# First block's feed-forwards: the first step as plain products in place of the seven-product scheme

## The chip, the cores and the metric

The kernel runs on one core of a Trainium2 chip. The metric is the device time of one execution in microseconds, taken over several runs. A core has a matrix engine (TensorE, PE), a vector engine (VectorE, DVE), an activation engine (ScalarE, ACT), a general engine (GpSimd, POOL) and a queue that starts most transfers (SyncE, SP). They run side by side and wait for one another by semaphores.

## The reference

A sequence of 512 tokens with 1024 channels goes through two blocks of two layers each. Every layer is a mixer (a gated delta rule, dilated window attention, sparse attention and others) and a feed-forward. The change touches the two feed-forwards of the first block, one after each of its mixers:

```python
def swiglu(h, w_in, w_out):
    gate, up = jnp.split(h @ w_in, 2, axis=-1)
    return (jax.nn.silu(gate) * up) @ w_out
...
h = (rms_norm(x, norm_ffn[layer]) * (1.0 + sc2) + sh2).astype(x.dtype)
x = x + g2 * swiglu(h, w_ffn_in[layer], w_ffn_out[layer])
```

`w_in` is 1024 x 5632 (2816 columns of gate and 2816 of up), `w_out` is 2816 x 1024, all in float32.

## The kernel before, in words

Activations are kept transposed: a tile is 128 channels (partitions) by 512 tokens, so `h` is 8 such tiles. The function `swiglu` (L1030) is one stage. Its first half makes 22 tiles of gate and 22 of up; its second multiplies by `w_out`. Weights come into two slots in turn (`c.slots[0]`, `c.slots[1]`); SP reloads a slot when the semaphore `done` says that TensorE has finished with it (L712). The weights of the first two steps are loaded in the stage before (`first_ffn_weights`).

**The seven products.** A step takes the weights of one tile of gate and one of up (both 1024 deep) and computes both tiles. Taken as a 2x2 by 2x2 product of blocks, this would be 8 block products; the class `SevenProducts` does it with 7, from sums of blocks of the weights and sums of blocks of `h` (a Winograd form of Strassen's scheme). Each block product is 4 matmuls of 256 columns, 28 a step, written out in `products` (L802 to L816; the matmul is L810) in the order P1, P2, P6, P7, P4, P5, P3. Who supplies what:

- P1 and P2 need only weights and `h` (in the first step TensorE waits for `h` tile by tile, semaphore `ready`).
- The sums of weights (`fold` in `gpsimd`, L735 to L741: four instructions a step) are made by POOL; P6 waits for them (`folded`).
- The sums of `h` (`sum_inputs`, L837 to L850) are made by DVE once in a stage: t1 (L844), t2 (L847), t3 (L848, written over the block b12 of `h` itself), t4 (L850). In the first step P6 waits for t2, P7 for t3, P4 for t4 (semaphore `t_in`).
- `combine` (L893 to L919) adds the seven products up on DVE into `gate` and `up`, as far as it can after P4 (`half_done`) and the rest after the step (`done`). The sums read PSUM banks 0 to 3 for even steps, 4 to 7 for odd ones.
- ACT takes the Silu of the gate (L1078), DVE multiplies it with up into `hidden` (L1114), and after each pair of steps adds sums of `hidden` (L885 to L890).

**Around the first step.** `Norm` makes `h`: TensorE spreads the inverse norm (L504), DVE scales tile by tile (L512), ACT adds the shift (L498). In the feed-forward of layer 0 alone there is extra work for the next mixer (`LayerAhead`): four small matmuls ahead of the first step (`make_rows`, L974), two copies and some transfers on ACT (L981, L985, L991), and multiplications of rows of `w_ada` on DVE (L1003, L1006) in the first eight pairs of steps. A semaphore `second_free` keeps the second step off the banks of `make_rows` until ACT has copied them.

The class already has a form for plain products in banks 0 and 1 (`whole_bank`), used by the second block's feed-forwards (L765), with `sum_inputs_early` (t1, t2, t4) and `sum_inputs_late` (t3, L870, after the plain steps have read `h`).

Of the kernel before, what the change touches and what calls it, by code (L numbers as in the profile page):

```python
# [18 lines left out]

F32 = mybir.dt.float32  # L20
ACT = mybir.ActivationFunctionType
LOG_AND_EXP, GELU = 6, 11
AX = mybir.AxisListType
ds = bass.ds

# [3 lines left out]
KT = D // P  # L29
# [19 lines left out]
FT = F1 // P  # L49
# [353 lines left out]
ADA_FIRST = 4  # L403
# [79 lines left out]
class Norm:  # L483
# [178 lines left out]
class SevenProducts:  # L662
# [18 lines left out]
    WHOLE = 2  # L681
# [44 lines left out]
    def landed_out(self, i, j):  # L726
        return i * (3 * 64) + (32 * self.KH + 64 * (j // 2 + 1))

    def gpsimd(self, pool, whole=False):

        c, nc = self.c, self.c.nc

        def fold(s, kc, before):
            b = lambda n: self.block(c.slots[s], n, kc)
            nc.gpsimd.tensor_tensor(b(self.S1), b(self.A21), b(self.A22), ALU.add).then_inc(self.folded, 1)  # L735
            pool.wait_ge(self.folded, before + 1)
            nc.gpsimd.tensor_tensor(b(self.S2), b(self.S1), b(self.A11), ALU.subtract).then_inc(self.folded, 1)
            pool.wait_ge(self.folded, before + 2)
            nc.gpsimd.tensor_tensor(b(self.S3), b(self.A11), b(self.A21), ALU.subtract).then_inc(self.folded, 1)  # L739
            pool.wait_ge(self.folded, before + 3)  # L740
            nc.gpsimd.tensor_tensor(b(self.S4), b(self.A12), b(self.S2), ALU.subtract).then_inc(self.folded, 1)  # L741
            pool.wait_ge(self.folded, before + 4)

        if whole:
            pool.sem_inc(self.folded, 4 * self.WHOLE)
        with pool.Fori(int(whole), self.KH) as i:
            for s in range(2):
                pool.wait_ge(self.loaded[s], self.landed_in(i))
                fold(s, 4, i * 8 + 4 * s)
        with pool.Fori(0, self.PAIRS // 2) as i:  # L750
            for j in range(6):
                pool.wait_ge(self.loaded[j % 2], self.landed_out(i, j))
                fold(j % 2, self.CHUNKS[j % 3][1], i * 24 + (4 * FT + 4 * j))
# [39 lines left out]
    def begin(self, pe):  # L793
        pe.sem_inc(self.done, 2)

    def tensor(self, pe, ready, second_free=None, whole=False):
        c, nc = self.c, self.c.nc
        ORDER = ((self.P1, self.A11, "b11"), (self.P2, self.A12, "b21"), (self.P6, self.S2, "t2"), (self.P7, self.S3, "t3"),
                 (self.P4, self.A22, "t4"), (self.P5, self.S1, "t1"), (self.P3, self.S4, "b22"))

        def products(s, bank, hidden, k0, kc, begin, end, folds, first=False):
            for r, b, name in ORDER:  # L802
                if r == self.P6:
                    pe.wait_ge(self.folded, folds)
                if first and r in (self.P6, self.P7, self.P4):
                    pe.wait_ge(self.t_in, {self.P6: 2, self.P7: 4 if whole else 3, self.P4: 3 if whole else 4}[r])
                for k in range(kc):
                    if first and not whole and r in (self.P1, self.P2):
                        pe.wait_ge(ready, k + 1 + (KT // 2) * (r == self.P2))
                    last = nc.tensor.matmul(c.ps[:, 4 * bank + r // 2, (r % 2) * self.HALF:(r % 2 + 1) * self.HALF],  # L810
                                            c.slots[s][:, b * 512 + k * P:b * 512 + (k + 1) * P],
                                            self.operand(hidden, name, k0 + k),
                                            start=(begin and k == 0 and (r % 2 == 0 or not hidden)), stop=(end and k == kc - 1 and (r % 2 == 1 or r == self.P4 or not hidden)))
                if r == self.P4 and end:
                    last.then_inc(self.half_done, 1)
            last.then_inc(self.done, 1)  # L816

        if not whole:
            self.begin(pe)
        with pe.Fori(int(whole), self.KH) as i:  # L820
            for s in range(2):
                pe.wait_ge(self.loaded[s], self.landed_in(i))
                pe.wait_ge(self.combined, i * 8 + (4 * s + 4))
                if s == 1 and second_free is not None:
                    pe.wait_ge(second_free, 2)
                products(s, s, False, 0, KT // 2, True, True, i * 8 + (4 * s + 4), first=(s == 0))
        with pe.Fori(0, self.PAIRS // 2) as i:
            for j in range(6):
                m, part = j // 3, j % 3
                k0, kc = self.CHUNKS[part]  # L830
                pe.wait_ge(self.loaded[j % 2], self.landed_out(i, j))
                if part == 0:
# [32 lines left out]
    def sum_inputs_late(self, dve):  # L865

        h, nc, N = self.c.h, self.c.nc, KT // 2
        b12, b22 = h[:, 0:N, self.HALF:S], h[:, N:KT, self.HALF:S]
        dve.wait_ge(self.done, 2 + self.WHOLE)
        nc.vector.tensor_tensor(b12, b22, b12, ALU.subtract).then_inc(self.t_in, 1)  # L870

    def whole_taken(self, dve):
# [157 lines left out]
def swiglu(c, layer, ahead=None):  # L1030
    nc = c.nc
    w_in, w_out = c.ins["w_ffn_in"][layer, :, :], c.ins["w_ffn_out"][layer, :, :]
    with c.nc.sbuf_tensor(f"ffn_hidden{layer}", [P, FT, S], F32) as hidden:
        with c.stage(gate=[P, 2, S], up=[P, 2, S], diagonal=[P, S], square=[P, 2, S], sums_in=[P, 3, KT // 2, S // 2],
# [3 lines left out]
            WITH_AHEAD = ahead.HALVES if ahead is not None else 0  # L1038
# [16 lines left out]
            @block.gpsimd  # L1055
            def _(pool):
                if ahead is not None:
                    ahead.clear(pool)
                ffn.gpsimd(pool)

            @block.tensor
            def _(pe):
                norm.tensor(pe)
                if ahead is not None:
                    ahead.make_rows(pe)
                ffn.tensor(pe, norm.ready, None if ahead is None else ahead.rows_copied)
                if ahead is not None:
                    pe.wait_ge(ffn.combined, 4 * FT + 4 * (ffn.PAIRS - 1) + 8)
                    ahead.sum_tiles(pe)
                stats.tensor(pe)  # L1070
                stats.spread(pe, diagonal_ready)

            @block.scalar
            def _(act):
                def gates(i):
                    for s in range(2):
                        act.wait_ge(ffn.combined, i * 8 + (4 * s + 12))
                        nc.scalar.activation(gate[:, s, :], gate[:, s, :], ACT.Silu).then_inc(gated, 1)  # L1078

                if ahead is not None:  # L1080
                    ahead.load_table(act)
                norm.scalar(act)
                if ahead is not None:
                    ahead.load_half(act, 0, 0)
                    ahead.load_half(act, 1, 0)
                    ahead.keep_rows(act)
                    gates(0)
                    with act.Fori(0, ADA_FIRST - 1) as q:
                        for u in range(2):
                            act.wait_ge(ahead.taken, q * 2 + (u + 1))  # L1090
                            ahead.load_half(act, u, q * 512 + 512)
                            gates(q * 2 + (u + 1))
                with act.Fori(max(WITH_AHEAD - 1, 0), FT // 2) as i:
                    gates(i)
                for m in range(ffn.PAIRS):
                    for t in range(2):
                        act.wait_ge(added, 2 * m + t + 1)
                        stats.square_tile(act, 2 * m + t, t, c.x[:, m + t * ffn.PAIRS, :])
                stats.root(act)

            @block.vector
            def _(dve):
                dve.sem_inc(ffn.combined, 8)
                norm.vector(dve)
                ffn.sum_inputs(dve, norm.ready)

                def tiles(i, q=None, u=None):
                    for s in range(2):
                        ffn.combine_in(dve, i, s, gate[:, s, :], up[:, s, :])
                        if q is not None:  # L1110
                            ahead.scale_rows(dve, q, u, s)
# [3 lines left out]
                                                ).then_inc(ffn.multiplied, 1)  # L1115
                    ffn.sum_hidden(dve, i)

                if ahead is not None:
                    with dve.Fori(0, ADA_FIRST) as q:
                        for u in range(2):  # L1120
                            tiles(q * 2 + u, q, u)
                with dve.Fori(WITH_AHEAD, FT // 2) as i:
                    tiles(i)
                add = add_gated(c, layer, 5)
                stats.begin(dve)
# [2895 lines left out]
```

## Time and profile before

| | us |
|---|---|
| median of 3 runs | 4227.16 (4225.35 to 4227.64) |
| the profiled execution's own time | 4223.88 |
| its span in the profile | 4222.1 |
| TensorE matmul busy in the span | 4057.9 (96%) |
| mean granted TensorE clock | 0.977 of full |

The profile is of one execution. Its time stands 1.8 us above its span. A time in a row is counted from the start of the span. A float32 matmul of the program shows as two records of MATMUL, so the 28 matmuls of a step are 56 records. "PEclk" is the granted TensorE clock, 1.00 for 2.4 GHz and 0.50 for 1.2 GHz.

### The profile page before, as it was taken

Reading aid. Unit: us, or ns where it says so; the run is one execution under the profiler, and the core shown is the slowest. Engines: PE = TensorE matmul, PEld = TensorE weight load, DVE = VectorE, ACT = ScalarE, POOL = GpSimd, SP = SyncE. Lnnn points to the kernel's source line nnn. Section 1 sums busy time; section 2 is a strip of 40 time slices with the busy share of each in tenths; the row PEclk is TensorE's granted clock in tenths of the full one; section 3 lists DMA queues with packets and bytes.
Section 4 is the critical chain, followed back from the end, with each engine's and each line's share of the span. In section 5 each row is a group of like instructions: output and inputs, shape, how many; then the busy total and the mean of one; then the engine's idle time right before and its main releaser. Section 6 shows DMA issues by size and latency. Waiting matters only on the chain. (4 is left out here: it accounts for less than half of the span.)

```text
span 4222.1 us, 52376 instructions
## 1 busy us (share of the span) xinstructions
PE 4057.9 (96%) x19141; PEld 3022.5 (72%) x19141; DVE 1985.4 (47%) x3671; ACT 844.7 (20%) x1844; POOL 1133.9 (27%) x894
## 2 busy tenths in 40 slices
PE   7998999999999799999989999999999899999998
PEld 3446958887666488874578847888745788478887
DVE  2445544422332433223357625785324676247852
ACT  2332210001333201003340111111123401111110
POOL 0003414444000134420026300454300264004443
PEclk9998999999999799999999999999899999999999
DMA  6221214323432123244223331322351233312322
GB/s 227 61 59 35 80 55 131 108 85 101 136 106 65 45 80 89 85 110 87 43 53 90 80 90 50 90 83 84 92 103 38 58 81 90 90 50 80 89 85 75
DMA packets 622412, 352.28 MB, mean 83 GB/s; under 512 B 68714, under 2 KB 592267, under 8 KB 622260
## 3 DMA queue, kind: packets, MB, share of 16 engines
q1 hardware_dynamic: 607368, 327.46, 28.9%
q10 hardware_dynamic: 14892, 22.78, 1.6%
q8 instruction: 97, 1.59, 0.2%
q14 instruction: 55, 0.45, 0.0%
HBM read 340.22 MB, written 2.62 MB: 81 GB/s over the span
## 5 line engine op out<-in xcount | busy, mean ns | idle before, releaser
L810 PE MATMUL psum<-h_normed,weight_slot 128*128 128x256 f32 x2688 | 613.0, 381 | 1.8 <-ACT h_normed L498 1.7
L810 PEld LDWEIGHTS psum<-h_normed,weight_slot 128*128 128x128 f32 x2688 | 513.5, 191 | 75.3 <-issue 4.1
L735 POOL TENSOR_TENSOR weight_slot<-weight_slot 128x512 f32<-128x512 f32 (+1 forms) x132 | 171.6, 1300 | 871.1 <-DMA weight_slot<-in_w_ffn_in 286.7
L902 DVE COPY work<-psum 128x256 f32<-128x256 f32 x100 | 42.1, 421 | 594.2 <-PE psum L810 594.2
L3054 PE MATMUL psum<-sums_of_h,weight_slot 128*128 128x256 f32 x1280 | 282.8, 379 | 0.0
L3054 PEld LDWEIGHTS psum<-sums_of_h,weight_slot 128*128 128x128 f32 x1280 | 243.2, 190 | 33.1
L2635 PE MATMUL psum<-h_normed,weight_slot 128*128 128x512 f32 x576 | 252.9, 596 | 1.0 <-ACT raw L2821 1.0
L810 PE MATMUL psum<-sums_in,weight_slot 128*128 128x256 f32 x1056 | 242.4, 379 | 2.4 <-DVE sums_in L847 2.4
L810 PE MATMUL psum<-sums_hidden,weight_slot 128*128 128x256 f32 x1056 | 243.7, 379 | 0.0
L3945 DVE SCALAR_TENSOR_TENSOR u<-raw,vectors,u 128x511 f32<-128x511 f32 (+1 forms) x160 | 203.0, 1288 | 60.1 <-ACT u L3917 48.4
L1320 PE MATMUL psum<-h_normed,weight_slot 128*128 128x512 f32 x512 | 226.5, 597 | 1.6 <-PEq L202 1.6
L810 PE MATMUL psum<-sums_of_h,weight_slot 128*128 128x256 f32 x960 | 220.5, 379 | 3.4 <-POOL weight_slot L741 3.4
L810 PEld LDWEIGHTS psum<-sums_in,weight_slot 128*128 128x128 f32 x1056 | 200.6, 190 | 30.0 <-issue 2.8
L810 PEld LDWEIGHTS psum<-sums_hidden,weight_slot 128*128 128x128 f32 x1056 | 200.5, 190 | 27.7 <-POOL weight_slot L741 0.5
L3054 PE MATMUL psum<-h_normed,weight_slot 128*128 128x256 f32 x960 | 214.2, 379 | 3.3 <-PEq L202 3.3
L3264 DVE SCALAR_TENSOR_TENSOR o_conv<-padded,vectors,o_conv 128x512 f32<-128x512 f32 x240 | 207.7, 936 | 0.0
L810 PEld LDWEIGHTS psum<-sums_of_h,weight_slot 128*128 128x128 f32 x960 | 182.2, 190 | 28.9 <-POOL weight_slot L741 4.2
L3054 PEld LDWEIGHTS psum<-h_normed,weight_slot 128*128 128x128 f32 x960 | 182.2, 190 | 28.4 <-issue 3.7
L2635 PEld LDWEIGHTS psum<-h_normed,weight_slot 128*128 128x128 f32 x576 | 107.6, 190 | 132.4 <-issue 132.1
L1320 PEld LDWEIGHTS psum<-h_normed,weight_slot 128*128 128x128 f32 x512 | 96.2, 191 | 120.4 <-issue 120.4
L741 POOL TENSOR_TENSOR weight_slot<-weight_slot 128x512 f32<-128x512 f32 (+1 forms) x132 | 176.7, 1339 | 10.4
L739 POOL TENSOR_TENSOR weight_slot<-weight_slot 128x512 f32<-128x512 f32 (+1 forms) x132 | 176.4, 1336 | 10.3
(515 smaller groups left out, 6457.2 us busy)
## 6 DMA issues: line engine op xcount, KB each, us to landing
weight_slot<-in_w_ffn_in SPq DMA_DIRECT2D x88, 512.0 KB
weight_slot<-in_ffn_w_up SPq DMA_DIRECT2D x88, 512.0 KB
weight_slot<-in_w_gate SPq DMA_DIRECT2D x64, 512.0 KB
weight_slot<-in_w_in SPq DMA_DIRECT2D x40, 512.0 KB, 5.2
weight_slot<-in_dsw_w_in SPq DMA_DIRECT2D x36, 512.0 KB, 6.7
weight_slot<-in_gdn_w_in SPq DMA_DIRECT2D x32, 512.0 KB, 15.4
weight_slot<-in_w_ffn_out SPq DMA_DIRECT2D x64, 256.0 KB
tile_ahead<-in_w_ada SPq DMA_DIRECT2D x16, 1024.0 KB, 7.3
```

Of the source, the lines that this page charges most:

```text
L735: nc.gpsimd.tensor_tensor(b(self.S1), b(self.A21), b(self.A22), ALU.add).then_inc(self.folded, 1)
L739: nc.gpsimd.tensor_tensor(b(self.S3), b(self.A11), b(self.A21), ALU.subtract).then_inc(self.folded, 1)
L741: nc.gpsimd.tensor_tensor(b(self.S4), b(self.A12), b(self.S2), ALU.subtract).then_inc(self.folded, 1)
L810: last = nc.tensor.matmul(c.ps[:, 4 * bank + r // 2, (r % 2) * self.HALF:(r % 2 + 1) * self.HALF], c.slots[s][:, b * 512 + k * P:b * 512 + ...
L902: nc.vector.tensor_copy(u4, p(self.P1)).then_inc(self.link, 1)
L1320: last = nc.tensor.matmul(c.ps[:, t, :], c.slots[s][:, (t * KT + k) * P:(t * KT + k + 1) * P], c.h[:, k, :], start=(k == 0), stop=(k == KT ...
L2635: last = nc.tensor.matmul(c.ps[:, BANK_OF[t], :], c.slots[j % 2][:, (i * KT + k) * P:(i * KT + k + 1) * P], c.h[:, k, :], start=(k == 0), ...
L3054: last = nc.tensor.matmul(c.ps[:, 4 * s + r // 2, (r % 2) * self.HALF:(r % 2 + 1) * self.HALF], c.slots[s][:, b * 512 + k * P:b * 512 + (k ...
L3264: nc.vector.scalar_tensor_tensor(o_conv[:, t, :], padded[:, t, k:k + S], at, o_conv[:, t, :], ALU.mult, ALU.add).then_inc(tapped, 1)
L3945: ins = nc.vector.scalar_tensor_tensor(u[:, s, t, back:], of(s, t)[:, 0:S - back], tap(i, s, t, 2 - back), u[:, s, t, back:], ALU.mult, AL ...
```

## The change

In both feed-forwards of the first block the first step (slot 0) is done as 16 plain matmuls of 512 columns (8 tiles of `h`, each against the gate's and the up's weights) into PSUM banks 0 and 1. POOL makes no sums of weights for this step and DVE does not combine it: ACT reads the gate from PSUM, DVE multiplies up from PSUM with it. DVE makes t1, t2 and t4 beside it, and t3, which overwrites a block of `h`, after it. The order in which the second step waits for the sums is therefore P6: t2, P7: t3 as the fourth sum, P4: t4 as the third. The second step is written out ahead of the loop, and the loop over pairs of steps starts at 1. On ACT the table of Silu is loaded by an instruction of its own ahead of the first gate.

```diff
     def gpsimd(self, pool, whole=False, lead=False):
...
+        if lead:
+            pool.sem_inc(self.folded, 4)
+            pool.wait_ge(self.loaded[1], self.landed_in(0))
+            fold(1, 4, 4)
-        with pool.Fori(int(whole), self.KH) as i:
+        with pool.Fori(int(whole or lead), self.KH) as i:
...
+    def lead_step(self, pe, ready):
+        c, nc = self.c, self.c.nc
+        pe.wait_ge(self.loaded[0], self.landed_in(0))
+        for k in range(KT):
+            pe.wait_ge(ready, k + 1)
+            for g in range(2):
+                last = nc.tensor.matmul(self.whole_bank(0, g), self.tile_in(c, 0, g)[:, k, :], c.h[:, k, :],
+                                        start=(k == 0), stop=(k == KT - 1))
+        last.then_inc(self.done, 1)
+        pe.sem_inc(self.half_done, 1)
...
-                    pe.wait_ge(self.t_in, {self.P6: 2, self.P7: 4 if whole else 3, self.P4: 3 if whole else 4}[r])
+                    pe.wait_ge(self.t_in, {self.P6: 2, self.P7: 4 if late else 3, self.P4: 3 if late else 4}[r])
...
+        if lead:
+            self.lead_step(pe, ready)
+            pe.wait_ge(self.loaded[1], self.landed_in(0))
+            if second_free is not None:
+                pe.wait_ge(second_free, 2)
+            products(1, 1, False, 0, KT // 2, True, True, 8, first=True)
-        with pe.Fori(int(whole), self.KH) as i:
+        with pe.Fori(int(late), self.KH) as i:
...
-        dve.wait_ge(self.done, 2 + self.WHOLE)
+        dve.wait_ge(self.done, 2 + steps)
...
-                def gates(i):
-                    for s in range(2):
+                def gates(i, first=0):
+                    for s in range(first, 2):
...
+                def first_gates():
+                    load_table(nc, act, SILU)
+                    act.wait_ge(ffn.done, 3)
+                    nc.scalar.activation(gate[:, 0, :], ffn.whole_bank(0, 0), ACT.Silu).then_inc(gated, 1)
+                    gates(0, 1)
...
-                    gates(0)
+                first_gates()
+                if ahead is not None:
                     with act.Fori(0, ADA_FIRST - 1) as q:
...
-                with act.Fori(max(WITH_AHEAD - 1, 0), FT // 2) as i:
+                with act.Fori(max(WITH_AHEAD - 1, 1), FT // 2) as i:
...
-                ffn.sum_inputs(dve, norm.ready)
+                ffn.sum_inputs_early(dve, norm.ready)
+                ffn.sum_inputs_late(dve, 1)
+                def first_tile():
+                    dve.wait_ge(gated, 1)
+                    nc.vector.tensor_tensor(hidden[:, 0, :], ffn.whole_bank(0, 1), gate[:, 0, :], ALU.mult).then_inc(ffn.multiplied, 1)
+                    if ahead is not None:
+                        ahead.scale_rows(dve, 0, 0, 0)
+                    dve.wait_ge(ffn.multiplied, 1)
+                    dve.sem_inc(ffn.combined, 4)
+                    dve.sem_inc(ffn.link, 4)
...
+                first_tile()
                 if ahead is not None:
-                    with dve.Fori(0, ADA_FIRST) as q:
+                    tiles(0, 0, 0, first=1)
+                    tiles(1, 0, 1)
+                    with dve.Fori(1, ADA_FIRST) as q:
...
+                else:
+                    tiles(0, first=1)
-                with dve.Fori(WITH_AHEAD, FT // 2) as i:
+                with dve.Fori(max(WITH_AHEAD, 1), FT // 2) as i:
```

## Rows read from the trace of the kernel before

**Rows 1.** The page: the span, and the engines' busy time, share and instructions.

```profile
span 4222.1 us, 52376 instructions
PE 4057.9 (96%) x19141; PEld 3022.5 (72%) x19141; DVE 1985.4 (47%) x3671; ACT 844.7 (20%) x1844; POOL 1133.9 (27%) x894
```

**Rows 2.** Timeline, TensorE, layer 0: start, duration, engine, line, out<-in, records, idle before.

```profile
615.69 3.58 PE L974 MATMUL psum<-sums_hidden,bias_table 33*8 33x256 f32 x8 [0.40 <-DMA sums_hidden<-in_constants]
619.20 6.63 PE L810 MATMUL psum<-h_normed,weight_slot 128*128 128x256 f32 x16
625.67 1.89 PE L810 MATMUL psum<-sums_in,weight_slot 128*128 128x256 f32 x8
...
632.58 5.34 PE L810 MATMUL psum<-h_normed,weight_slot 128*128 128x256 f32 x24
...
644.66 5.34 PE L810 MATMUL psum<-h_normed,weight_slot 128*128 128x256 f32 x24
649.85 1.89 PE L810 MATMUL psum<-sums_in,weight_slot 128*128 128x256 f32 x8
```

**Rows 3.** Timeline, TensorE, layer 1.

```profile
1468.76 5.22 PE L810 MATMUL psum<-h_normed,weight_slot 128*128 128x256 f32 x16 [1.69 <-ACT h_normed L498]
1476.39 1.97 PE L810 MATMUL psum<-sums_in,weight_slot 128*128 128x256 f32 x8 [2.41 <-DVE sums_in L847]
...
1483.79 5.34 PE L810 MATMUL psum<-h_normed,weight_slot 128*128 128x256 f32 x24
```

**Rows 4.** Windows, TensorE: stretch, length, busy (records), granted clock, DMA share, GB/s.

```profile
625.00:625.50 0.50, 0.50 (x4) 0.86 1.04 397
1471.50:1472.00 0.50, 0.50 (x4) 0.86 0.00 0
1888.00:1888.50 0.50, 0.50 (x2) 0.93 1.29 250
3055.00:3055.50 0.50, 0.50 (x2) 0.57 1.04 309
```

**Rows 5.** Timeline, TensorE: 512-column matmuls at full clock, and twice after a norm.

```profile
1438.92 20.87 PE L244 MATMUL psum<-o_windows,weight_slot 128*128 128x512 f32 x48 [0.50 <-DMA weight_slot<-in_dsw_w_out]
1882.96 16.50 PE L2696 MATMUL psum<-h_normed,weight_slot 128*128 128x512 f32 x32 [1.32 <-DVE h_normed L512]
3052.47 15.43 PE L2696 MATMUL psum<-h_normed,weight_slot 128*128 128x512 f32 x32 [1.55 <-DVE h_normed L512]
```

**Rows 6.** Timeline, the other engines, around the first step of layer 0.

```profile
616.11 5.33 ACT L498 ACTIVATE h_normed<-h_normed,modulation 128x512 f32<-128x512 f32 x8 [4.40 <-DVE h_normed L512]
622.24 2.10 DVE L847 TENSOR_TENSOR sums_in<-h_normed,sums_in 128x1024 f32<-128x1024 f32 x1
623.33 2.13 POOL L741 TENSOR_TENSOR weight_slot<-weight_slot 128x512 f32<-128x512 f32 x1
624.25 2.28 DVE L848 TENSOR_TENSOR h_normed<-h_normed 128x1024 f32<-128x1024 f32 x1
626.42 1.28 ACT L1078 ACT_TABLE_LOAD   x1 [3.63 <-issue]
634.65 25.17 SPq L712 DMA_DIRECT2D weight_slot<-in_w_ffn_in  x6
635.62 0.63 ACT L1078 ACTIVATE gate<-gate 128x512 f32<-128x512 f32 x1 [7.92 <-DVE gate L899]
636.02 0.75 DVE L1006 SCALAR_TENSOR_TENSOR tile_rows<-tile_ahead,cond,tile_rows 128x512 f32 x1
636.69 0.69 DVE L1114 TENSOR_TENSOR ffn_hidden<-up,gate 128x512 f32 x1
644.24 1.27 POOL L741 TENSOR_TENSOR weight_slot<-weight_slot 128x512 f32<-128x512 f32 x1
```

**Rows 7.** Timeline, TensorE: code entered anew.

```profile
888.12 3.62 PE L810 MATMUL psum<-ffn_hidden,weight_slot 128*128 128x256 f32 x16
...
3336.73 3.69 PE L3054 MATMUL psum<-h_normed,weight_slot 128*128 128x256 f32 x16 [1.64 <-PEq L202]
```

More of the change, by code:

```diff
@@ L21 @@
 ACT = mybir.ActivationFunctionType
-LOG_AND_EXP, GELU = 6, 11
+LOG_AND_EXP, GELU, SILU = 6, 11, 18
 AX = mybir.AxisListType
@@ L727, in landed_out, with gpsimd @@
         return i * (3 * 64) + (32 * self.KH + 64 * (j // 2 + 1))
-    def gpsimd(self, pool, whole=False):
+    def gpsimd(self, pool, whole=False, lead=False):
         c, nc = self.c, self.c.nc
@@ L794, in begin, with tensor @@
         pe.sem_inc(self.done, 2)
-    def tensor(self, pe, ready, second_free=None, whole=False):
+    def lead_step(self, pe, ready):
         c, nc = self.c, self.c.nc
+        pe.wait_ge(self.loaded[0], self.landed_in(0))
[6 more added lines that the diff above has]
+        pe.sem_inc(self.half_done, 1)
+    def tensor(self, pe, ready, second_free=None, whole=False, lead=False):
+        c, nc = self.c, self.c.nc
+        late = whole or lead
         ORDER = ((self.P1, self.A11, "b11"), (self.P2, self.A12, "b21"), (self.P6, self.S2, "t2"), (self.P7, self.S3, "t3"),
@@ L805, in products @@
                 if first and r in (self.P6, self.P7, self.P4):
-                    pe.wait_ge(self.t_in, {self.P6: 2, self.P7: 4 if whole else 3, self.P4: 3 if whole else 4}[r])
+                    pe.wait_ge(self.t_in, {self.P6: 2, self.P7: 4 if late else 3, self.P4: 3 if late else 4}[r])
                 for k in range(kc):
-                    if first and not whole and r in (self.P1, self.P2):
+                    if first and not late and r in (self.P1, self.P2):
                         pe.wait_ge(ready, k + 1 + (KT // 2) * (r == self.P2))
@@ L863, in sum_inputs_early, with sum_inputs_late @@
         nc.vector.tensor_tensor(t4, b21, t2, ALU.subtract).then_inc(self.t_in, 1)
-    def sum_inputs_late(self, dve):
+    def sum_inputs_late(self, dve, steps=WHOLE):
         h, nc, N = self.c.h, self.c.nc, KT // 2
         b12, b22 = h[:, 0:N, self.HALF:S], h[:, N:KT, self.HALF:S]
-        dve.wait_ge(self.done, 2 + self.WHOLE)
+        dve.wait_ge(self.done, 2 + steps)
         nc.vector.tensor_tensor(b12, b22, b12, ALU.subtract).then_inc(self.t_in, 1)
@@ L1058, in _ @@
                     ahead.clear(pool)
-                ffn.gpsimd(pool)
+                ffn.gpsimd(pool, lead=True)
             @block.tensor
@@ L1065, in _ @@
                     ahead.make_rows(pe)
-                ffn.tensor(pe, norm.ready, None if ahead is None else ahead.rows_copied)
+                ffn.tensor(pe, norm.ready, None if ahead is None else ahead.rows_copied, lead=True)
                 if ahead is not None:
@@ L1104, in _, with tiles @@
                 norm.vector(dve)
-                ffn.sum_inputs(dve, norm.ready)
-                def tiles(i, q=None, u=None):
-                    for s in range(2):
+                ffn.sum_inputs_early(dve, norm.ready)
[8 more added lines that the diff above has]
+                    dve.sem_inc(ffn.link, 4)
+                def tiles(i, q=None, u=None, first=0):
+                    for s in range(first, 2):
                         ffn.combine_in(dve, i, s, gate[:, s, :], up[:, s, :])
```

## The prediction

> **What bounds the kernel now.** I read the page's engine shares first: the matrix engine's matmuls cover 4057.9 of 4222.1 us, 96% [rows 1]. So the time changes by what moves on TensorE and by little else. Next came TensorE's timeline around the start of each of the two feed-forwards, because the edit sits there, then the granted clock in half-microsecond windows, then the other engines' timelines beside it.
>
> A steady step of seven products takes 644.66 - 632.58 = 12.08 us: 56 records, 0.216 us each [rows 2]. From P6 of the first step (625.67) TensorE shows no idle time until the stage ends. The row at 632.58 holds 8 records of P3 (8 x 0.216 = 1.73 us), so the second step starts at 634.31. The first step took 634.31 - 619.20 = 15.11 us. Where did 3.03 us go? Not to a visible wait: 16 records took 6.63 us because they ran at half clock. The four small matmuls ahead show it already: 3.58 us for 8 records of 256 columns, about 0.43 each, which is twice 0.216 [rows 2]. The clock is at 1.2 GHz until the window 625.00 to 625.50, whose mean is 0.86; that puts the rise at 625.14, so 5.94 us of the first step were at half clock [rows 4]. In layer 0 the sums of `h` (t2 ends at 624.34) and of the weights (the last ends at 625.46) come just before P6 wants them [rows 6]. They cost almost nothing only because half clock kept P1 and P2 busy until then.
>
> In layer 1 the step starts at 1468.76, when the first tile of `h` is there. The clock rises at 1471.64 (same reading, 0.86), so 2.88 us are at half clock [rows 4]. P1 and P2 are through sooner and TensorE idles 2.41 us for t2, until 1476.39; the second step starts at 1483.79 + 1.73 = 1485.52 [rows 3]. The first step took 16.76 us.
>
> **The change, part by part.**
>
> *The plain step itself.* It is 16 matmuls of 512 columns, 32 records. 48 such records at full clock took 20.87 us; less the last one's tail (0.60 long against the pitch) that is (20.87 - 0.60) / 47 = 0.431 us each [rows 5]. So 32 x 0.431 = 13.79 us, against 12.08 for seven products: 1.71 us more work a layer. Half clock adds half of its stretch. Waits inside it: none. It needs one tile of `h` per two matmuls, 1.72 us, while ACT delivers one each 0.67 us (5.33 us for 8) [rows 6]. Its start does not move: in layer 0 the four small matmuls stand ahead until 619.20, in layer 1 the first tile of `h`. So second step's start = first start + 13.79 + half of the stretch at half clock.
>
> With this trace's own stretches: layer 0 619.20 + 13.79 + 2.97 = 635.96 against 634.31, 1.65 us later. Layer 1 1468.76 + 13.79 + 1.44 = 1483.99 against 1485.52, 1.53 us earlier. Sum +0.12 us. The old step's length hardly depends on the stretch, since P6 waited for sums; the new one's does.
>
> The nearest rows to the new step are two groups with the same count and shape, 32 records of 512 columns right after a norm: 16.50 and 15.43 us [rows 5]. Their stretches at half clock are 5.11 us (1882.96 to 1888.07) and 2.96 us (3052.47 to 3055.43) [rows 4]; my formula plus a tail of 0.17 gives 16.52 and 15.44, so it holds. Four stretches are seen: 5.94, 5.11, 2.96, 2.88. Their mean, 4.22, gives 619.20 + 15.90 = 635.10 (+0.79) and 1468.76 + 15.90 = 1484.66 (-0.86): sum -0.07. Both short (2.9): +0.13 and -1.52, so -1.4. Both long (5.94): +1.65 and 0.00, so +1.7. I take 0, and -1.4 to +1.7 as the ends.
>
> The Trainium skill ("TensorE: Matmul & The Clock Gate", section "What's actually happening") says that the throttle's activity watch runs free of the kernel, so the moment of the rise varies from run to run. By it the trace's own 5.94 and 2.88 are not tied to their layers and the sum is the -0.07 of the mean; were they tied, it is +0.12. One profile can't tell; both round to nothing.
>
> *Sums of `h` beside it and behind it.* t1, t2 and t4 start when ACT has the eighth tile (616.11 + 5.33 = 621.44). At no more than 2.28 us each the three are there by 628.3 [rows 6], and P6 of the second step wants them at 635.1 + 3.45 (P1 and P2) = 638.6: hidden, with 10 us of cover. That cover, not shorter work, is what removes the 2.41 us stall. t3 must wait for the plain step's end. It took 2.28 us beside POOL [rows 6], so it ends some 2.4 us into the second step; P7 comes after 24 records, 5.2 us in. Cost 0 with 2.8 us to spare; without that cover it would cost at most its 2.28 us. The wait sits at the head of DVE's queue. Behind it stand the product of gate and up (0.69 us), two scalings in layer 0 (0.75 at most each) and the combination of the second step [rows 6]. These are through 2.4 + 0.7 + 1.5 = 4.6 us into the second step; the combination can start after P4, 40 records or 8.6 us in. So nobody waits.
>
> *ACT.* The table load (1.28 us, now at 626.42) stays in the shadow of the plain step; the first gate (0.63 us) has TensorE's end as its wait, and behind it in the queue stands only the second step's gate [rows 6]. The third step wants the first's banks at 12.1 us into the second, and has them at about 4.6. ACT's and DVE's reads of PSUM have no row in just this form; I bound them by 0.63 and 0.69 and by twice that, which the 7 us of slack hide either way.
>
> *POOL and SP.* Four folds a layer go (some 1.3 us each, off the path), and slot 1's four start that much sooner. SP's reload of slot 0 still goes out at the step's end (634.65 in layer 0), folded by 645.51; P6 of the third step comes at 649.85 [rows 2, 6]. All three hang on the same event and move together, so the 4.3 us of slack stay. No DMA is added.
>
> *Combining the first step* (seven sums and copies on DVE) goes; it was covered by the next step. Worth 0.
>
> *Code written out once more, loops from 1.* The trace enters a fresh loop at 888.12 (inputs to outputs) with no idle time; the dearest such entry is 1.64 us at 3336.73, charged to the engine's own sequencer [rows 7]. So 0 to 1.64 us a layer, 0 to 3.3 in all. I take 0, since the entry at 888.12 is this very function's, entered out of dense matmuls.
>
> **Sum.** The profiled time was 4223.88, 1.8 above its span, and 3.3 below the median of 3; the change adds 0 to it. On the median that is 4227.2 us. Most of what decides is a trade: 1.7 us more work a layer against stalls of 0.0 and 2.4 us and a first step stretched to the sums' pace anyway.
>
> **The rivals.**
>
> 1. *The clock is no cost to the plain step* (wide, dense matmuls raise it at once). Then 619.20 + 13.79 = 632.99 (-1.32) and 1482.55 (-2.97): -4.3, giving 4222.9. For it: fewer, longer records. Against it: rows of just this shape ran 5.11 and 2.96 us at half clock.
> 2. *Code fetch takes the stall's place, slower.* At the boundary from the written-out second step to the loop TensorE waits for its instructions, 1.64 us a layer: +3.3, giving 4230.5. It decides once the fetch outlasts the matmuls that are queued. The Trainium skill ("Runtime: NRT & Kernel Launch", section "Instruction fetch mechanics") says that a taken branch to code not yet fetched stalls until it is. Against it is the entry at 888.12, and that the six-step output loop jumps back again and again without an idle row; for it is 3336.73.
> 3. *The clock stays low through the whole plain step.* 32 x 0.862 = 27.6 us: 646.8 against 634.3 and 1496.3 against 1485.5, +23.3, giving 4250.5. It decides if the rise needs something that these 16 matmuls lack. The same two groups of 32 speak against it.
> 4. *The late sum is not covered*: DVE is held by something else at the plain step's end, and P7 waits up to 2.28 us a layer: +4.6, 4231.8. It needs DVE over 2.8 us late, and DVE has nothing to do between 628.3 and that end.
>
> That the change doesn't do what it says: all it needs is that the plain step sits in banks 0 and 1 while the second writes 4 to 7, which the code has.
>
> **How the numbers follow.** Forecast as above, -1.4 to +1.7 us: 0.80. Rival 1: 0.06. Rival 2: 0.07. Rival 3: 0.01. Rival 4: 0.02. The last 0.04 is for something elsewhere that I don't see, either way. A change of 0.2% is 8.5 us, about what a measurement of this kernel can tell from none; the forecast and rivals 1, 2 and 4 all stay inside it, only rival 3 and the unseen leave it. Hence faster 0.02, same 0.95, slower 0.03. Range: below, rival 1's 4222.9; above, rival 2 with the spread of the runs (up to 1 us over rival 2's 4230.5): 4222.9 to 4231.5.
>
> **What would show it.** The plain step's 32 records last 15.4 to 16.8 us in both layers, and the second step's P6 follows P2 with no idle time. Layer 0's second step starts later than 634.3, or as late, and layer 1's earlier than 1485.5 (counted from the same first matmul). The late sum runs within 2.5 us of the plain step's end, and POOL shows four operations fewer a layer. An idle row "<-PEq" at the third step speaks for rival 2, a wait of P7 for DVE for rival 4, a plain step near 13.9 us for rival 1. The prediction is wrong if the time moves by over 4 us either way.

## The result, and the profile after

The changed kernel takes 4234.69 us (median of 19, 4229.26 to 4238.56) against 4226.7 (median of 19), ratio 1.0018 [1.0012, 1.0024]: about 8 us more, 3.2 us above the top of the range. Its profiled execution took 4232.74 us, the one before 4223.88, so the two traces differ by 8.9 us. Means, with their standard errors, are used below where several kernels are compared. The kernel before was measured five times, with means of 4226.1 to 4226.6 (standard errors up to 0.4); differences below are taken from the mean of all its runs, 4226.4 +- 0.2. After has 4234.2 +- 0.6, which is 7.8 us more.

The page of after, its span and shares, answers to [rows 1]:

```profile
span 4231.0 us, 52115 instructions
PE 4064.7 (96%) x19093; PEld 3015.0 (71%) x19093; DVE 1984.0 (47%) x3655; ACT 831.9 (20%) x1834; POOL 1118.3 (26%) x886
```

TensorE's timeline of after, layer 0 and then layer 1 (columns as in [rows 2, 3]):

```profile
619.70 15.72 PE L807 MATMUL psum<-h_normed,weight_slot 128*128 128x512 f32 x32
635.26 3.62 PE L827 MATMUL psum<-h_normed,weight_slot 128*128 128x256 f32 x16
...
645.62 5.34 PE L827 MATMUL psum<-h_normed,weight_slot 128*128 128x256 f32 x24
650.80 1.89 PE L827 MATMUL psum<-sums_in,weight_slot 128*128 128x256 f32 x8
...
1470.36 17.03 PE L807 MATMUL psum<-h_normed,weight_slot 128*128 128x512 f32 x32 [1.69 <-ACT h_normed L498]
1487.23 3.62 PE L827 MATMUL psum<-h_normed,weight_slot 128*128 128x256 f32 x16
1490.68 1.89 PE L827 MATMUL psum<-sums_in,weight_slot 128*128 128x256 f32 x8
```

The step itself did what was forecast. First step: 635.26 - 619.70 = 15.56 us against 15.11 in layer 0, 1487.23 - 1470.36 = 16.87 against 16.76 in layer 1, together +0.56 us. P6 follows P2 without idle time in both; the 2.41 us stall [rows 3] is gone; the third step is entered (within the row at 645.62) without an idle row. The windows of after on the two steps give the granted clock (columns as in [rows 4], all engines):

```profile
617.00:625.00 8.00, 8.00 (x16) 2.98 (x15) 7.14 (x9) 5.61 (x9) 1.35 (x2) 0.61 0.38 118
1470.00:1480.00 10.00, 9.64 (x16) 4.14 (x17) 7.75 (x10) 6.11 (x9) 1.63 (x2) 0.67 0.00 0
```

0.61 over 8 us puts the rise from 1.2 to 2.4 GHz at 623.24, so 3.54 us of the step at half clock: 13.79 + 1.77 = 15.56, as measured. 0.67 over 10 us puts it at 1476.6, so 6.2 us at half clock: 13.79 + 3.1 = 16.9. VectorE and GpSimd beside the second step of layer 0:

```profile
635.46 1.23 DVE L893 TENSOR_TENSOR h_normed<-h_normed 128x1024 f32<-128x1024 f32 x1 [10.13 <-PE psum L807]
636.60 0.68 DVE L1140 TENSOR_TENSOR ffn_hidden<-psum,gate 128x512 f32<-128x512 f32 x1
...
645.24 1.27 POOL L741 TENSOR_TENSOR weight_slot<-weight_slot 128x512 f32<-128x512 f32 x1
```

The late sum is through 1.4 us into the second step, before the 5.2 at which P7 wants it; slot 0's last fold ends at 646.51, 4.3 us before P6 of the third step (650.80), as forecast.

So where do the 8.9 us arise? The same places of the program, read off both timelines, tell it. TensorE, before:

```profile
2410.16 1.89 PE L3054 MATMUL psum<-h_normed,weight_slot 128*128 128x256 f32 x8
...
2451.77 3.69 PE L3726 MATMUL psum<-o_nsa,weight_slot 128*128 128x512 f32 x8 [1.95 <-DVEq L3761]
...
2657.17 1.99 PE L810 MATMUL psum<-sums_of_h,weight_slot 128*128 128x256 f32 x8 [1.68 <-POOL weight_slot L741]
...
3820.24 3.62 PE L810 MATMUL psum<-h_normed,weight_slot 128*128 128x256 f32 x16
3825.54 1.99 PE L810 MATMUL psum<-sums_of_h,weight_slot 128*128 128x256 f32 x8 [1.68 <-POOL weight_slot L741]
3827.37 1.89 PE L810 MATMUL psum<-h_normed,weight_slot 128*128 128x256 f32 x8
```

and after:

```profile
2411.04 1.89 PE L3099 MATMUL psum<-h_normed,weight_slot 128*128 128x256 f32 x8
...
2452.65 5.39 PE L3771 MATMUL psum<-o_nsa,weight_slot 128*128 128x512 f32 x8 [1.95 <-DVEq L3806]
...
2660.02 2.90 PE L827 MATMUL psum<-sums_of_h,weight_slot 128*128 128x256 f32 x8 [1.96 <-POOL weight_slot L741]
...
3825.32 3.72 PE L827 MATMUL psum<-h_normed,weight_slot 128*128 128x256 f32 x16 [0.60 <-DMA weight_slot<-in_ffn_w_up]
3831.53 3.63 PE L827 MATMUL psum<-sums_of_h,weight_slot 128*128 128x256 f32 x8 [2.49 <-POOL weight_slot L741]
3834.95 1.99 PE L827 MATMUL psum<-h_normed,weight_slot 128*128 128x256 f32 x8
```

Both changed feed-forwards lie before 1900. At 2410 after is only 0.88 us behind. The rest arises in the second block, whose source the change doesn't touch:

- At 2452 come 1.70 us more, where eight records run largely at half clock (5.39 against 3.69 us; the granted clock over 2452 to 2460 is 0.79 against 1.00).
- At 2657 the distance is 2.85 us, and a slow row follows (2.90 against 1.99 us). Ahead of the wait at 3825 it is about 4.5 us; it rises and falls on the way.
- At 3825, in the last feed-forward, come about 3.1 us: 0.60 of waiting for a weight load, 0.81 more for its folds (2.49 - 1.68), and 1.64 because the eight records then run at half clock (3.63 against 1.99; granted clock over 3831 to 3836 0.66 against 1.00).
- The last 1.3 us come behind 4196, around the small matmuls of the final norm (16 records 2.73 against 1.95 us, two records of 512 columns 2.08 against 1.60).

### The profile page after: what moved, and what is told of

The parts are those of the page before. It is cut to its first block and busy times, and to the rows that moved or that the text cites. A ratio compares the mean times of both kernels' runs of the same rounds, so it can differ in the third digit from the quotient of the medians.

```text
span 4231.0 us, 52115 instructions
## 1 busy us (share of the span) xinstructions
PE 4064.7 (96%) x19093; PEld 3015.0 (71%) x19093; DVE 1984.0 (47%) x3655; ACT 831.9 (20%) x1834; POOL 1118.3 (26%) x886
## 3 DMA queue, kind: packets, MB, share of 16 engines
q8 instruction: 98, 1.61, 0.2%
## 5 line engine op out<-in xcount | busy, mean ns | idle before, releaser
L827 PE MATMUL psum<-h_normed,weight_slot 128*128 128x256 f32 x2624 | 594.8, 379 | 0.6 <-DMA weight_slot<-in_ffn_w_up 0.6
L827 PEld LDWEIGHTS psum<-h_normed,weight_slot 128*128 128x128 f32 x2624 | 499.4, 190 | 70.1 <-issue 2.0
L735 POOL TENSOR_TENSOR weight_slot<-weight_slot 128x512 f32<-128x512 f32 (+1 forms) x130 | 167.2, 1286 | 894.4 <-DMA weight_slot<-in_w_ffn_in 302.1
L827 PE MATMUL psum<-sums_in,weight_slot 128*128 128x256 f32 x1008 | 231.3, 379 | 0.0
L3099 PE MATMUL psum<-h_normed,weight_slot 128*128 128x256 f32 x960 | 214.2, 379 | 3.6 <-PEq L202 2.0
L3309 DVE SCALAR_TENSOR_TENSOR o_conv<-padded,vectors,o_conv 128x512 f32<-128x512 f32 x240 | 216.4, 972 | 0.0
L827 PEld LDWEIGHTS psum<-sums_in,weight_slot 128*128 128x128 f32 x1008 | 191.5, 190 | 26.0
L3099 PEld LDWEIGHTS psum<-h_normed,weight_slot 128*128 128x128 f32 x960 | 182.2, 190 | 28.7 <-issue 4.0
L2680 PEld LDWEIGHTS psum<-h_normed,weight_slot 128*128 128x128 f32 x576 | 107.6, 190 | 132.4 <-issue 132.1
L1365 PEld LDWEIGHTS psum<-h_normed,weight_slot 128*128 128x128 f32 x512 | 96.6, 192 | 121.2 <-issue 121.2
L741 POOL TENSOR_TENSOR weight_slot<-weight_slot 128x512 f32<-128x512 f32 (+1 forms) x130 | 172.7, 1329 | 10.2
L737 POOL TENSOR_TENSOR weight_slot<-weight_slot 128x512 f32<-128x512 f32 (+1 forms) x130 | 171.8, 1321 | 10.2
```

Source lines behind the costliest of these rows:

```text
L1365: last = nc.tensor.matmul(c.ps[:, t, :], c.slots[s][:, (t * KT + k) * P:(t * KT + k + 1) * P], c.h[:, k, :], start=(k == 0), stop=(k == KT ...
L2680: last = nc.tensor.matmul(c.ps[:, BANK_OF[t], :], c.slots[j % 2][:, (i * KT + k) * P:(i * KT + k + 1) * P], c.h[:, k, :], start=(k == 0), ...
L3099: last = nc.tensor.matmul(c.ps[:, 4 * s + r // 2, (r % 2) * self.HALF:(r % 2 + 1) * self.HALF], c.slots[s][:, b * 512 + k * P:b * 512 + (k ...
L3309: nc.vector.scalar_tensor_tensor(o_conv[:, t, :], padded[:, t, k:k + S], at, o_conv[:, t, :], ALU.mult, ALU.add).then_inc(tapped, 1)
```

## The experiments

The theory formed from this: the change makes the engines' programs longer, so all code behind it sits at another place, and its fetches fall at other moments. The compiled programs (64 bytes an instruction) hold, before and after: TensorE 25136 and 25493 instructions (+357), VectorE 3395 and 3462 (+67), ScalarE 2425 and 2427 (+2), GpSimd 1057 and 1067 (+10), SyncE the same. The rival: something the changed stages do (weights loaded or slots freed at other moments) is carried on. The page of before has the instruction queues; after has 98 and 1.61 on q8, and the same q14:

```profile
q8 instruction: 97, 1.59, 0.2%
q14 instruction: 55, 0.45, 0.0%
```

1.59 MB in 97 transfers is 16.4 KB each, 256 instructions; q14 moves 8.2 KB, 128 instructions. The counts say which program each queue carries. q8 follows TensorE's: 97 transfers with 101 instructions more than before (e8 below), 98 with 256 more (e12), 99 with 512 more (e1, e9). q14 follows the three others: 640 instructions more on them (e9) make 60 transfers of 55. (e1, e2 and so on are the experiments in their order.)

If positions matter, a shift by whole transfers should cost nothing. Idle waits on a semaphore long since at its value do the shifting (two in the source compile to one instruction); these kernels compute all that the reference does. Below, "filled" means lengthened up to whole transfers, counted from the kernel before, and "shifted" means lengthened by a part of one. TensorE's fill in the changed kernel (77 and 78 in the two layers, so that +512 in all stands for +357):

```
 for k in range(KT):
     for g in range(2):
         last = nc.tensor.matmul(...)
+        if 2 * k + g < 15:
+            for _ in range(2 * (self.pads // 15 + (2 * k + g < self.pads % 15))):
+                pe.wait_ge(self.loaded[0], self.landed_in(0))
```

**TensorE's code behind the change shifted by two whole transfers.**

> The kernel after, with 77 and 78 idle semaphore waits added on TensorE inside the two plain steps (after each matmul, where the array is busy 0.86 us and the sequencer is free). The program of TensorE grew by 357 instructions in the change (25136 to 25493); with the pads by 512. One code transfer of queue q8 carries 1.59 MB / 97 = 16.4 KB, 256 instructions of 64 bytes, so all code behind the two feed-forwards lies again as in the kernel before, measured in such blocks. Theory A (where TensorE's code blocks end decides which weight loads they collide with, the +8 us are that): this runs at the time before within the stage's own -1.4 to +1.7 us, 4225 to 4229 us, ratio 0.9997 to 1.0005, and the 0.60 us wait for the load ahead of the second block's last seven-product steps is gone. Theory B (the plain step itself, by waits or clock, costs it): 4234 to 4235, as the kernel after. Theory C (code of DVE, ACT or POOL has moved, not TensorE's): 4234 too.

Measured: 4228.6, ratio 1.0007 [0.9998, 1.0016], mean 4229.0 +- 0.7. Of the 7.8 us between the means, 5.2 went.

**The kernel before, with TensorE's code shifted as in the change.** 179 and 178 instructions of idle waits between the matmuls of the output products:

```
                 if hidden and k < kc - 1:
+                    for _ in range(2 * self.pad_after()):
+                        pe.wait_ge(self.t_in, 4)
...
+            ffn.pads = (179, 178)[layer]
```

> The kernel before, with 179 and 178 idle semaphore waits added to TensorE's program inside the output loops of the two feed-forwards (some 1.6 at a matmul, the array is busy 0.43 us at each). No arithmetic changes; the code behind them is moved by 357 instructions, as the change moves it. Theory A: most of the +8 us appear without the change, 4231 to 4235 us, ratio 1.001 to 1.002. Theory B and C: the time before, 4226 to 4228, unless the waits themselves cost something, which would show as longer output steps (12.08 us now) in the two stages.

Measured: 4229.39, 1.0006 [0.9997, 1.0015], mean 4229.6 +- 0.7: +3.2, a part of the loss without any of the change's work.

**The change in one layer alone, TensorE filled.** As e1, with `lead=layer in (0,)` and `(1,)`.

> The plain first step in layer 0 alone, TensorE's code filled up to a whole block (77 waits in the step). By the prediction's sum 0.1 to 1.7 us later: 4227 to 4228.5. Theory A: just that. Theory B: up to half or more of the +8 us, 4230 or more. Theory C: part of the +8, since DVE's program grows by 51 of the 67 instructions here.

> The plain first step in layer 1 alone, TensorE's code filled up to a whole block (78 waits in the step). By the prediction's sum 1.5 us earlier to 0: 4225.2 to 4226.7. Theory A: just that. Theory B: the rest of the +8 us, if layer 0 alone doesn't show it. Theory C: a small part (16 of DVE's 67 instructions).

Measured: layer 0 4227.52, 1.0003 [0.9994, 1.0012], mean 4227.2 +- 0.8; layer 1 4226.2, 0.9999 [0.999, 1.0008], mean 4225.8 +- 0.6. Their sum over 4226.4 is +0.2 +- 1: the stages themselves trade evenly, as forecast. Only TensorE's code is filled in these two; e9 fills every engine's.

**The changed kernel again**, to see that the 8 us stay.

> The kernel after itself, unchanged, so that the kernels with moved code are compared with it on one chip. 4233 to 4236 us, ratio 1.0013 to 1.0025. By theory A its profile shows again the late load at the second block's last feed-forward: TensorE waits some 0.5 us for the DMA ahead of the first seven-product step and 2.5 us for POOL before P6, against 0 and 1.68 us before.

Measured: 4234.77 (10 runs), 1.0019 [1.001, 1.0029], mean 4233.8 +- 0.9.

**The kernel before, with all four engines' programs as long as in the change**, and none of its arithmetic:

```
+            ffn.pads = (179, 178)[layer]        # TensorE
+            ffn.idle_pool = (5, 5)[layer]       # GpSimd, in the output loop
...
+                        for _ in range(2 * (0, 2)[layer] * (m == 0 and t == 0)):
+                            act.wait_ge(ffn.t_in, 4)
...
+                idle_dve = (51, 16)[layer]      # spread behind the sums of squares
```

> The kernel before, with idle waits on four engines in the first block's two output loops, so that each program has exactly the length of the kernel after: TensorE 25493 instructions, DVE 3462, ACT 2427, POOL 1067. No arithmetic of the change is in it. Theory A (only TensorE's code position counts): as the one with TensorE's code alone moved, 4229 to 4230 us, and the 5 to 6 us between it and the kernel after stay unexplained. Theory A2 (the position of all engines' code counts): 4232 to 4235, the whole loss. Theory B (the plain step costs it, and filling up its code merely took that back by chance): at most 4229.

Measured: 4234.26, 1.0019 [1.001, 1.0029], mean 4234.5 +- 0.9. Some 0.8 us of it are its own waits on VectorE at the end of layer 0's stage. This settles it: 7.3 of the 7.8 us are there without the change's work.

**VectorE filled too, in the changed kernel** (77 and 112 instructions, in four places behind the sums of squares).

> The kernel after with TensorE's program filled up to whole blocks of 256 instructions as before, and DVE's up to 128 more in layer 0 and 128 more in layer 1 (queue q14 moves 0.45 MB / 55 = 8.2 KB a transfer, 128 instructions). Theory A: as with TensorE alone, 4228.6. Theory A2: down to the stages' own cost, 4226 to 4227.5.

Measured: 4236.2, 1.0021 [1.0012, 1.003], mean 4235.1 +- 1.0: the expectation missed. The waits themselves stand in the way, since the sums of squares close the stage. VectorE's timeline of that kernel, the last of them in each layer (idle, charged to the engine's own issuing):

```profile
1026.62 0.69 DVE L570 TENSOR_TENSOR diagonal<-diagonal,square 128x512 f32<-128x512 f32 x1 [1.29 <-issue]
...
1879.98 0.69 DVE L570 TENSOR_TENSOR diagonal<-diagonal,square 128x512 f32<-128x512 f32 x1 [2.17 <-issue]
```

These two make 3.5 us; of the 6.1 us by which e7 is above e1, some 3 are not explained. With waits so placed, this run says little of positions; e9 has them elsewhere.

**TensorE shifted by 101 alone** (357 = 256 + 101), all in layer 1: `pads = (0, 101)`.

> The kernel before with 101 idle waits on TensorE in layer 1's output loop alone: 357 is 256 + 101, so behind it each block of code ends where it ends with 357. Theory A: the late load at the second block's last feed-forward is there (wait for the DMA about 0.5 us, for POOL about 2.6), and the time is 4228 to 4231. If only the total length or the plain step mattered, the profile would show 0 and 1.7 us there and the time would be 4226.6.

Measured: 4229.26, 1.0005 [0.9996, 1.0014], mean 4228.9 +- 0.5, +2.5: 101 instructions cost about as much as 357 (+3.2).

**The changed kernel with every engine shifted by whole transfers**, the waits where the engines idle anyway (TensorE 25648 = 25136 + 512, VectorE +256, ScalarE +128, GpSimd +256):

```
+            ffn.idle_pool = (122, 122)[layer]                # behind the output loop
+            ffn.pads = (77, 78)[layer]
...
+                        for _ in range(2 * (0, 126)[layer] * (m == 0 and t == 1)):
+                            act.wait_ge(ffn.t_in, 4)
...
+                        for _ in range(2 * (77, 112)[layer] * (m == 0)):
+                            dve.wait_ge(ffn.t_in, 4)
```

> The kernel after with idle waits on all four engines that grew, so that every program is longer than in the kernel before by whole blocks (TensorE by 512 instructions, DVE, POOL by 256, ACT by 128), this time where the engine stands idle: DVE after the first of each two combinations of the output loop (25 us of waiting there), POOL behind its last fold. In the earlier kernel with DVE filled up the waits stood in the stage's tail and cost 1.3 and 2.2 us there by its profile. Theory A2 (the position of all engines' code is the loss): 4226 to 4228, and no late load at the second block's last feed-forward. Theory D (besides the blocks' ends something else of the length of DVE's program or of the new stages matters): 4230 to 4233.

Measured: 4226.36, 1.0001 [0.9992, 1.001], mean 4227.1 +- 0.6. What is left is +0.7 +- 0.7 us, with all of the change's work still there. This and e6 are the two ends of the proof.

**VectorE alone, and GpSimd with ScalarE, in the kernel before** (+67; +10 and +2).

> The kernel before with DVE's program alone moved as the change moves it (51 and 16 idle waits, in DVE's idle time in the two output loops). All engines' code moved gave 4234.5 in the mean and TensorE's alone 4229.6, so 5 us are left, of which 0.8 were those waits' own. Theory A2 with DVE as the carrier: 4229 to 4231. If POOL's code is the carrier: 4226.6.

> The kernel before with POOL's program 10 instructions longer and ACT's 2, as the change has them. If DVE's code is the carrier: 4226.6. If POOL's or ACT's: 4229 to 4231.

Measured: 4225.56, 0.9998 [0.9989, 1.0007], mean 4225.4 +- 0.7; and 4229.59, 1.0007 [0.9998, 1.0016], mean 4229.9 +- 0.5. VectorE's 67 add nothing; the second pair's 12 add 3.5 us.

**Control: 256 on TensorE in the kernel before**, `pads = (128, 128)`, more waits than the 101 of e8, which cost 2.5 us.

> Control: the kernel before with 256 idle waits on TensorE in the two output loops, one whole block of code, placed like the 357 that moved it by a block and 101. Theory A: the waits cost nothing and the blocks end where they did behind layer 1, 4226 to 4227.5. If the waits themselves cost the 3 us: 4228.5 to 4229.

Measured: 4226.14, 1.0001 [0.9992, 1.001], mean 4226.6 +- 0.5. Between dense matmuls the waits cost nothing measurable; what counts is the remainder by 256.

**GpSimd alone and ScalarE alone, and the best version.** What was open: which of the two carries the 3.5 us, and whether the change in layer 1 alone, all engines filled, gains.

```
+        for _ in range(2 * self.idle_pool):     # behind GpSimd's output loop
+            pool.wait_ge(self.folded, 4)
```

> The kernel before with POOL's program alone 10 instructions longer (idle waits behind its last fold in both stages). If POOL's code carries the second part: 4229 to 4230.5. If ACT's: 4226 to 4227.

> The kernel before with ACT's program alone 2 instructions longer. If ACT's code carries the second part: 4229 to 4230.5. If POOL's: 4226 to 4227. If both come out near 4226.5, the two must be moved together.

> The plain first step in layer 1 alone, every program filled up to whole blocks. By the prediction's sum the step is worth 1.5 us to 0: 4225.0 to 4226.5, which is faster than both kernels or the same as before, and nothing of the +8 us is left.

Measured: GpSimd 4229.73, 1.0009 [1.0, 1.0018], mean 4229.8 +- 0.3; ScalarE 4226.23, 1.0 [0.9991, 1.0009], mean 4226.5 +- 0.8; layer 1 alone 4225.36, 0.9997 [0.9988, 1.0006], mean 4224.8 +- 0.5. Ten more instructions on GpSimd carry the whole of it, 3.4 us. The last is the lowest mean of all kernels, but its interval still includes a ratio of 1.

All kernels by what is shifted, as the mean's distance from 4226.4 us:

| TensorE shifted | GpSimd shifted | kernels |
|---|---|---|
| no | no | e9 +0.7, e10 -1.0, e12 +0.2, e14 +0.1, e15 -1.6 |
| no | by one layer's share | e3 +0.8, e4 -0.6 |
| yes | no | e2 +3.2, e8 +2.5 |
| no | yes | e1 +2.6, e11 +3.5, e13 +3.4; e7 +8.7 with its waits |
| yes | yes | the change +7.8, again (e5) +7.4, e6 +8.1 |

The intervals of the ratio are wider than these standard errors: of the kernels with one engine shifted, those of e1, e2, e8, e11 and e13 reach down to 1.000 or just below. One such run alone would prove little; the claim rests on the groups, and on the traces below.

### Where a shifted fetch costs

*TensorE's part* sits in the last feed-forward. SyncE and GpSimd of the kernel before, from the issue of the load to the first fold (the first row's duration spans six issues):

```profile
3813.69 21.94 SPq L712 DMA_DIRECT2D weight_slot<-in_ffn_w_up  x6
3819.18 1.27 POOL L735 TENSOR_TENSOR weight_slot<-weight_slot 128x512 f32<-128x512 f32 x1 [20.12 <-DMA weight_slot<-in_ffn_w_up]
```

The same of after:

```profile
3817.99 25.30 SPq L712 DMA_DIRECT2D weight_slot<-in_ffn_w_up  x6
3825.27 1.84 POOL L735 TENSOR_TENSOR weight_slot<-weight_slot 128x512 f32<-128x512 f32 x1 [21.90 <-DMA weight_slot<-in_ffn_w_up]
```

From issue to first fold it takes 5.49 us before and 7.28 after. The DMA view of after, the half microsecond from 3821.0 and then the whole stretch from issue to fold (packets, MB, share of 16 engines), shows what else is under way:

```profile
q1 hardware_dynamic: 335, 0.16, 109.9%
q8 instruction: 1, 0.02, 11.9%
...
q1 hardware_dynamic: 2080, 1.05, 51.1%
q8 instruction: 1, 0.02, 0.8%
```

One instruction transfer falls amid the load. It is one packet, and 11.9% of 16 engines in 0.5 us is 0.95 us, on one engine. Half-microsecond windows give the load's packets from 3820.5 on as 328, 335, 315, 290, 154, 22, 21, 21, 10; before, they go from 287 through 209 and 8 to nothing. 335 / 16 is 21, so the rate after 3823.0 is that of one engine of the 16, and the fold waits for the last packet. That this is the engine that moved the instruction packet isn't shown by name; the view doesn't tell engines apart. In before, q8's transfer comes 8 us behind the first fold. So the load ends 1.8 us late, of which the packet's own 0.95 is seen; the rest isn't explained. What follows takes more: the longer wait at the folds, and then half clock.

Over all 17 kernels' traces this place has two forms only:

```
                                            issue to fold   wait at P6   8 records of P6
TensorE shifted by 101 beyond a multiple
of 256 (after, its repeat, e2, e6, e8)        7.1 - 7.3      2.5 - 2.7      3.1 - 3.7 us
all twelve others                             5.5 - 5.8      1.7 - 1.9      2.0
```

The DMA view between issue and first fold shows a transfer of q8 in each of the five, and in none of the twelve.

One of the twelve is e9, the change with every engine filled; its SyncE, GpSimd and TensorE:

```profile
3816.45 22.00 SPq L714 DMA_DIRECT2D weight_slot<-in_ffn_w_up  x6
3822.14 1.27 POOL L737 TENSOR_TENSOR weight_slot<-weight_slot 128x512 f32<-128x512 f32 x1 [20.32 <-DMA weight_slot<-in_ffn_w_up]
3828.36 1.99 PE L834 MATMUL psum<-sums_of_h,weight_slot 128*128 128x256 f32 x8 [1.74 <-POOL weight_slot L743]
```

0.60 + 0.81 + 1.64 = 3.05 us in the trace of after against +3.2 and +2.5 in the runs that shift TensorE alone (e2, e8). Here place, size and cause meet. That filling TensorE in the changed kernel takes off 5.2 us (e1), more than shifting it alone adds, is not explained; the two differ by 2.0 +- 1.2.

*GpSimd's part* is less well placed. TensorE's timeline of e13 (GpSimd shifted), then of e14 (ScalarE shifted), at the entry of the second block's projections and at the one after:

```profile
2169.07 5.38 PE L3058 MATMUL psum<-h_normed,weight_slot 128*128 128x256 f32 x16 [1.95 <-PEq L202]
...
2452.45 5.39 PE L3730 MATMUL psum<-o_nsa,weight_slot 128*128 128x512 f32 x8 [1.95 <-DVEq L3765]
```

```profile
2170.00 3.69 PE L3056 MATMUL psum<-h_normed,weight_slot 128*128 128x256 f32 x16 [1.65 <-PEq L202]
...
2451.69 3.69 PE L3728 MATMUL psum<-o_nsa,weight_slot 128*128 128x512 f32 x8 [1.95 <-DVEq L3763]
```

The wait at 2169 is 1.95 or 1.96 us in all seven kernels whose GpSimd code is 10 longer (after, its repeat, e1, e6, e7, e11, e13) and 1.64 to 1.68 in the ten others: 0.3 us that GpSimd's position sets. The 1.7 us of half clock behind either wait come and go less strictly: the first is in e2, e6, e7, e11 and e13, not in after; the second in after, its repeat, e1, e2, e6, e7, e9, e11 and e13. So GpSimd's 3.4 us are shown as a total, and of their place only the 0.3 and, by single executions, two stretches at half clock. That a slightly longer idle time tips the clock is a guess, not shown: at 2452 the wait is 1.95 either way, and the clock differs. Which fetch, if any, lies behind it isn't shown, so for GpSimd the mechanism stays open.

## Why the prediction was wrong

*The plain step*: right. 13.79 us plus half of the stretch gave both lengths to 0.1 us with the stretches of this trace, 3.5 and 6.2 us. Tied to their layers they were not: they came the other way round, and with 6.2 us layer 1's second step started 0.11 us later than before, not earlier as forecast. The sum was +0.56, inside -1.4 to +1.7.

*Sums of `h`, late sum, ScalarE, GpSimd, SyncE, combination*: right. All hidden; the late sum took 1.23 us instead of 2.28, with no GpSimd row beside it. With every engine's code filled, the change costs +0.7 +- 0.7 us (e9). Rivals 1 and 3 are out by the step's 15.6 and 16.9 us, rival 4 by P7, which waits for nothing. (Rival 4's 4231.8 lay above the stated top of 4231.5; it played no part.)

*"Code written out once more, loops from 1"*: this step failed. It was priced at 0 (0 to 3.3) as a stall at the loop's entry, and there it is 0. But its cost wasn't there. The written-out steps make TensorE's program 357 instructions longer and GpSimd's 10, and everything behind, over half the kernel, is fetched at other moments. With TensorE's shift a fetch meets a weight load that is awaited, for +3; GpSimd's shift is worth +3.4; both together, with nothing of the change's work, +8 (e6). Rival 2 had the right resource and the wrong place: it looked where the new code is entered, not at what all later code does.

The trace of before held the material: 97 instruction transfers of 16.4 KB, the length of the added code, and weight loads of 1 MB that end close ahead of their use. Which transfer would meet which load couldn't have been forecast to the microsecond, but the bound could: a term of some us either way for moved code, not tied to a place. By the prediction's own sign, a move of over 4 us either way, it is wrong. It also took 0.2%, 8.5 us, for what a measurement can tell from none. The ratio of 1.0018 lies just inside that, but its interval, 1.0012 to 1.0024, leaves out 1: 8 us can be told from none, so that bound was too coarse.

The Trainium skill ("Runtime: NRT & Kernel Launch", section "Instruction fetch mechanics") says that crossing a boundary of 16 KiB in the code costs "one DMA tail-bump, mostly hidden". The block size agrees with q8's 16.4 KB a transfer, not with q14's 8.2 KB. Hidden is not what the transfer at 3821 was: TensorE's waits there are for the weight load that the transfer met and for its folds, and 3.05 us were lost. For the other transfers no run here shows one by one whether they were hidden.

Open: the second half of the 1.8 us that the load lost; where GpSimd's 3.4 us arise beyond 0.3, and by what; why the clock fell at 2452 and in the final norm, and not in the trace of before; 0.7 us by which e6 exceeds the sum of the single shifts and its own waits (8.1 - 3.2 - 3.4 - 0.8 = 0.7, with errors of about 1); and 3 us of e7.

## What to carry to other kernels

In a kernel near its bound, code added early is an edit of everything behind it: forecast a term of a few us either way for the moved fetches, and widen the range by it, even where the edit's own stages come out at zero. Before a difference of 0.2% is put down to what an edit does, run the old kernel with its programs as long as the new ones (idle waits in a place with slack), and the new one filled up to whole instruction transfers. A weight load of which the last packet is awaited is the place to look for a collision: compare issue to first use in both traces.

## What was not expected of the hardware

- One instruction transfer of 16.4 KB took 0.95 us amid a weight load, and the load was 1.8 us late (7.28 against 5.49 us).
- A wait of 0.60 us for that load grew to 3.05 us: the wait for the folds grew by 0.81, and a granted clock that fell after it added 1.64.
- 256 instructions of idle waits on TensorE between dense matmuls cost nothing (4226.6 against 4226.4), while 19 to 28 of them in a row on VectorE in the norm's chain cost 1.3 to 2.2 us.
- Ten more instructions on GpSimd cost 3.4 us, 67 on VectorE and 2 on ScalarE nothing that could be measured.
